# The attention stages in pairs of heads, and three of four value rows of one tile on TensorE

## What is computed

```python
def mla(q, k, v):                       # first block, causal
    s = q @ k.T / sqrt(96);  p = softmax(where(causal, s, -inf))
    return p @ v

def peer(x):                            # 128 experts per token
    s1, s2 = q[..., :64] @ keys_1.T, q[..., 64:] @ keys_2.T
    eidx, gates = top16_of_top16_by_top16(s1, s2)
    act = gelu(einsum('td,tkd->tk', x, peer_u[eidx]))
    return einsum('tk,tkd->td', gates * act, peer_v[eidx])

def nsa(q, ...):                        # second block, per head
    o_c = masked_softmax(q @ k_cmp.T / 8, cmp_end <= t) @ v_cmp   # 31 compressed keys
    o_s = masked_softmax(q @ k_sel.T / 8, causal) @ v_sel         # 512 tokens: every block is chosen
    o_w = masked_softmax(q @ k_win.T / 8, causal) @ v_win
    return g0 * o_c + g1 * o_s + g2 * o_w
```

## Time and profile before

| | us |
|---|---|
| median of the 3 runs shown | 3436.53 (3432.90 to 3439.03) |
| the profiled execution | 3432.37 |
| its span | 3431.0 |
| busy TensorE | 2454.4 (72%) |
| busy VectorE | 1890.6 (55%) |
| busy ScalarE | 456.1 (13%) |
| busy GpSimd | 1311.4 (38%) |

### The profile page before, as it was taken

One profiled execution on the slowest core, in us unless ns is written; L12 is line 12 of the kernel. 1 busy time (PEld: TensorE's weight loads), 2 busy tenths in 40 slices (PEclk: granted clock), 3 DMA queues, 4 the chain that ended last, 5 costly groups with the idle time before them and its releaser, 6 DMA issues. The chain is left out here.

```text
span 3431.0 us, 24950 instructions
## 1 busy us (share of the span) xinstructions
PE 2454.4 (72%) x8300; PEld 1594.3 (46%) x8300; DVE 1890.6 (55%) x3669; ACT 456.1 (13%) x1214; POOL 1311.4 (38%) x1041
## 2 busy tenths in 40 slices
PE   6998930365847543003959998897679979799989
PEld 3547630234526522002647686763356534466544
DVE  1511169887676778997777656666554442212100
ACT  1201000012101000000023210110122100122110
POOL 0000004767466877347664345885431241000000
PEclk9998965685767866555855579999755789855699
DMA  4221406898688999669897569999863699510176
GB/s 138 92 85 65 162 21 196 308 384 294 225 338 285 402 331 363 194 209 335 327 352 226 174 234 400 371 401 401 308 228 90 212 398 336 189 37 0 63 268 226
DMA packets 291711, 829.17 MB, mean 242 GB/s; under 512 B 23568, under 2 KB 30144, under 8 KB 290816
## 3 DMA queue, kind: packets, MB, share of 16 engines
q0 software_dynamic: 148416, 539.79, 43.8%
q1 hardware_dynamic: 139872, 283.19, 22.7%
q10 hardware_dynamic: 3296, 4.60, 0.4%
HBM read 825.40 MB, written 2.10 MB: 241 GB/s over the span
## 5 line engine op out<-in xcount | busy, mean ns | idle before, releaser
L306 POOL DMA_INDIRECT picks_rows<-peer_u_dram,expert x512 | 698.2, 1364 | 821.0 <-DVE expert L1441 506.1
L306 POOL DMA_INDIRECT picks_rows<-peer_v_dram,expert x512 | 605.7, 1183 | 770.1 <-DVE h L369 655.6
L363 DVE CUSTOM_DVE_ANT_0 picks_rows<-picks_rows,xn 128x1024 f32<-128x1024 f32 x512 | 616.7, 1223 | 178.8 <-DMA picks_rows<-peer_u_dram,expert 173.7
L369 DVE SCALAR_TENSOR_TENSOR h<-picks_rows,picks_weight,h 128x1024 f32<-128x1024 f32 x512 | 655.0, 1279 | 101.5 <-ACT aT L2031 47.7
L637 PE MATMUL psum<-identity_sb,n_scaled 128*128 128x128 f32 (+1 forms) x104 | 23.6, 405 | 327.0 <-DVE n_scaled L622 327.0
L447 PE MATMUL psum<-weight_ring,hnT 128*128 128x512 f32 (+4 forms) x576 | 238.6, 576 | 23.5 <-DMA weight_ring<-w_in_dram 11.9
L1727 PE MATMUL psum<-weight_ring,aT 128*128 128x512 f32 x512 | 224.4, 600 | 8.6 <-DMA weight_ring<-w_ff_dram 6.4
L931 DVE TENSOR_REDUCE na_negmax<-psum 128x1 f32<-128x15 f32 (+6 forms) x192 | 74.3, 387 | 254.6 <-PE psum L836 254.4
L835 PE MATMUL psum<-nsa_kT_sb,qT 64*128 64x128 f32 (+3 forms) x256 | 181.2, 809 | 0.0
L447 PEld LDWEIGHTS psum<-weight_ring,hnT 128*128 128x128 f32 (+1 forms) x576 | 106.9, 188 | 153.8 <-issue 140.4
L637 PEld LDWEIGHTS psum<-identity_sb,n_scaled 128*128 128x128 f32 (+1 forms) x104 | 19.4, 218 | 332.7 <-issue 293.0
(11 more groups left out here) (357 smaller groups left out, 3422.4 us busy)
## 6 DMA issues: line engine op xcount, KB each, us to landing
weight_ring<-w_ff_dram SPq DMA_DIRECT2D x48, 2048.0 KB, 16.0
weight_ring<-w_in_dram SPq DMA_DIRECT2D x44, 2048.0 KB, 13.2
weight_ring<-w_proj_nsa_dram SPq DMA_DIRECT2D x6, 2048.0 KB, 7.9
weight_ring<-w_out_dram SPq DMA_DIRECT2D x6, 2048.0 KB, 18.7
weight_ring<-w_ret_out_dram SPq DMA_DIRECT2D x4, 2048.0 KB, 7.9
weight_ring<-w_mix_out_dram SPq DMA_DIRECT2D x4, 2048.0 KB, 18.2
weight_ring<-w_peer_q_dram SPq DMA_DIRECT2D x4, 2048.0 KB, 13.2
picks_rows<-peer_u_dram,expert POOLq DMA_INDIRECT x512, 9.3
```

The source lines that it names most:

```text
L306: pool.indirect_dma_start(out=self.rows[:, n % GATHERS, :], out_offset=None, in_=table, in_offset=bass.IndirectOffsetOnAxis(ap=self.expert ...
L363: ins = nc.vector.tensor_tensor_reduce(out=row, in0=row, in1=self.x[t], scale=1.0, scalar=0.0, op0=ALU.mult, op1=ALU.add, accum_out=self.d ...
L369: ins = nc.vector.scalar_tensor_tensor(out=h, in0=row, scalar=self.weight[:, t % 2, k:k + 1], in1=h, op0=ALU.mult, op1=ALU.add)
```

## The change

**Attention.** Items come in pairs, two heads of the same tile and branch. The mask matmul is gone: q is scaled by a negative number, and VectorE adds a mask of 0 and large positive numbers to the scores in PSUM and takes the minimum in one operation (`tensor_tensor_reduce`, out in place). ScalarE's exponential has scale −1 and that minimum as bias. VectorE then takes the reciprocal of each row sum and scales the probabilities themselves, by the gate too. The value product is swapped: values are stationary (64 columns), the turned probabilities move (128 columns), and the output comes out turned, the two heads in the two halves of the partitions, all three branches summed in one PSUM bank; ScalarE copies a whole bank to `oT`. VectorE's output steps, the buffers `o` and `mla_o`, and the stages `to_…` and `to2_…` are gone. In the second block q, k and the compressed k stand on 128 partitions: head h has rows 64·(h%2) and up, which takes each k turned twice (`turn_twice`) and q turned in blocks of 128. Score banks are 4 (2 for more than 512 keys), probability buffers 4 and 4.

**Picks.** `on_pe` is true for three of four v picks of tile 1, 96 of 1024. For each GpSimd writes a diagonal matrix of weights (identity x weight, 128 x 128, four buffers, 5 picks behind the gathers), and TensorE adds the row by two matmuls of 512 columns to PSUM banks 6 and 7; `fold` adds the two banks to h at the end. Other stages have 6 banks now. The counts in `SHARES` are new, and picks are placed in finer turns in some stages. Up to `sel2` 399 − 17 = 382 picks are placed; `sel2`, `sel3` and `drain_0` take 51 + 51 + 28, of which 36 + 39 + 21 are TensorE's.

```diff
-BANKS = 8
+BANKS = 6
 SHARES = {
-    ... "ma2_1": 28, "ma3_1": 28, "rp_1": 43, "tr_1": 7, "re_1": 19, "rn_1": 8, "to_1": 4, "m1_1": 71, "mix_1": 24, ...
-    "sel2": 43, "sel3": 42, "drain_0": 28, ... "cmp2_0": 31, ... "na2_0": 89, "to2_0": 3, "m2_0": 42, ... "ff12_0": 61, "ff22_0": 60,
-    ... "cmp2_1": 17, ... "na2_1": 29, "to2_1": 1, "m2_1": 16, ... "ff12_1": 18, "ff22_1": 19, ...
+    ... "ma2_1": 26, "ma3_1": 27, "rp_1": 35, "tr_1": 7, "re_1": 58, "rn_1": 9, "m1_1": 55, "mix_1": 18, ...
+    "sel2": 51, "sel3": 51, "drain_0": 28, ... "cmp2_0": 41, ... "na2_0": 81, "m2_0": 46, ... "ff12_0": 50, "ff22_0": 49,
+    ... "cmp2_1": 24, ... "na2_1": 35, "m2_1": 10, ... "ff12_1": 11, "ff22_1": 12, ...
-def on_pe(k):
-    return False
+def on_pe(t, k):
+    return t == 1 and k % 4 > 0
...
+    def fold(self, dve, t):
+        ...
+        dve.wait_ge(self.taken["dve"], self.dve_done_by(end))
+        dve.wait_ge(self.taken["pe"], pe_picks)
+        for c, bank in enumerate(V_BANKS):
+            h = self.g.h[:, t, 512 * c:512 * c + 512]
+            self.g.nc.vector.tensor_tensor(h, h, self.g.psum[:, bank, :], ALU.add).then_inc(self.sum_added, 1)
...
+def turn_twice(g, bank, columns, src, rows):
+    for part in (0, HD):
+        mm = g.nc.tensor.matmul(g.psum[part:part + HD, bank, columns], src, g.identity[0:rows, 0:rows], start=True, stop=True)
...
-            nc.tensor.matmul(scores(i)[:, at:end], it.q, it.kT, start=True, stop=False)
-            return nc.tensor.matmul(scores(i)[:, end - it.bias.shape[1]:end], g.identity[:], it.bias, start=False, stop=True)
+        def value(pe, s):
+            for j in pair(s):
+                it = items[j]
+                pe.wait_ge(*s_copied.after(j + 1))
+                ...
+                for m, (_, keys, v) in enumerate(it.blocks):
+                    mm = nc.tensor.matmul(values(j), v, probsT[0:keys, j % 4, P * m:P * m + P], start=it.start and m == 0,
+                                          stop=it.stop and m == len(it.blocks) - 1)
+                mm.then_inc(s_values.sem, 1)
...
+            for s in range(steps + 2):
+                if wide:
+                    turn(pe, s - 1)
+                    score(pe, s)
+                else:
+                    score(pe, s)
+                    turn(pe, s - 1)
+                value(pe, s - 2)
+                g.picks.add(pe, 2 * min(s, steps))
...
+            for s in range(steps):
+                for i in pair(s):
                     dve.wait_ge(*s_scores.after(i + 1))
-                    nc.vector.tensor_reduce(negmax[:, i % 4:i % 4 + 1], scores(i), AX_X, ALU.max, negate=True).then_inc(s_max.sem, 1)
+                    nc.vector.tensor_tensor_reduce(out=scores(i), in0=scores(i), in1=items[i].mask, scale=1.0, scalar=-LOWEST,
+                                                   op0=ALU.add, op1=ALU.min, accum_out=least[:, i % 8:i % 8 + 1]).then_inc(s_least.sem, 1)
+                g.picks.use(dve)
+                for i in pair(s):
+                    it, p = items[i], probs[:, i % 4, 0:items[i].keys]
+                    f = factor[:, i % 8:i % 8 + 1]
+                    dve.wait_ge(*s_exp.after(i + 1))
+                    if it.seen is not None:
+                        nc.vector.tensor_tensor(p, p, it.seen, ALU.mult)
+                    link(nc.vector.reciprocal(f, rowsum[:, i % 8:i % 8 + 1]))
+                    ...
+                        ins = nc.vector.tensor_scalar(p, p, f, it.gate, ALU.mult, ALU.mult)
+                    ins.then_inc(s_normed.sem, 1)
                 g.picks.use(dve)
```

## The result

| | us |
|---|---|
| before, median of 4 | 3437.78 (3432.90 to 3445.01) |
| changed, median of 4 | 3163.11 (3153.72 to 3168.80) |
| ratio | 0.9197, 95% interval 0.9167 to 0.9227 |
| forecast | 3170, range 3100 to 3262 |

A forecast was written before the change was run, and what follows sets the result against it. Attention stages na2_0 to na2_2 were taken as TensorE's at 1.2 GHz, selection as VectorE's, ff22_0 and m1_1 as the DMA's. Terms −8 − 41 − 23 − 18 − 64 − 114 = −268 from 3432 gave 3164, rounded to 3170; range 3100 to 3262.

The forecast's parts named there:

- na2_2: Second block's last attention stage, no picks: masks go, paired scores overlap, clock rises to 1.00; 202 to 91 us, −111.
- na2_1: Second block's middle attention stage: VectorE's own work plus 35 picks, 108 us with gaps for 167, −59.
- na2_0: Second block's first attention stage: VectorE takes over as the bound, 208 us with gaps for 233, −25.
- To 519: Start of the kernel to 519 us: ma0_0 loses masks and output steps and to_0 goes, −8.
- sel2 to drain_0: Selection stages, 250 us: 96 picks go to GpSimd and TensorE, gathers 1.55 apart, 227 us, −23.
- GpSimd is the new bound: Rival for the selection: unpriced diagonals slow gathers to 1.9 to 2.2 us each, total 3210 to 3245; chance 0.12.
- my signs of being wrong: Listed signs included clock 0.50 in na2_2, minimum above 1.0 us, diagonals over 0.6 us, paired scores one after another.
- 519–1328: Stretch from 519 to 1328 us: fewer picks, masks gone, scores overlapping, to_1 gone, picks shifted (+7); −41.
- Second block, stages around: Stages around na2_0, 1578–2396: 22 more picks ahead +24, ff12_0 and ff22_0 −13; whole stretch −18.
- A cold attention: Rival: attention's clock stays at 1.2 GHz, na2_2 149 to 160 us, na2_1 118, total 3245; chance 0.18.
- an exposed chain: Rival: each attention step's chain of 3.7 us, passing VectorE twice, is not hidden; slower, above 3437; chance 0.04.
- no overlap: Rival: paired heads' scores do not overlap, 11.2 us a pair, +15 to +25, total 3190; within the forecast's 0.66.

The follow-up runs named there:

- split_pair: The changed kernel with each score of a pair on TensorE followed by the turn of one item, so the two scores stand apart: 3230.22 us, na2_2 114.0.
- mask_back: The changed kernel with the mask matmul put back behind each score on TensorE: 3229.09 us, na2_2 112.6.
- before_no_mask: The kernel before without its mask matmuls, masks left out of the result: 3352.03 us, na2_2 176.9.
- fill_start: The changed kernel with spare full-width matmuls on TensorE after the first and second step of each attention stage: 3152.11 us, ma0_0 31.5.
- act_diag: The changed kernel with the 96 diagonals made by ScalarE instead of GpSimd: 3118.60 us, ratio to before 0.9082, sel2 to drain_0 222.
- attn_only: The changed kernel with all picks on VectorE and the pick counts of the kernel before: 3175.15 us, ratio to before 0.9244.
- dve_picks: The changed kernel with its new counts but all 1024 picks on VectorE: 3174.16 us, ratio to before 0.9237, sel2 to drain_0 271.

## Why the prediction was right, and where it was wrong

**na2_2 (−111 forecast, −117).** The mechanism was right: the overlap of the halves, the high clock, three engines of nearly the same load. split_pair and mask_back each take away the neighbourhood of the scores and give back 29 and 28 us; the clock is 0.89 in the change. Of the sizes, the overlap is complete (1.13 for four against 1.12 for two), where I had taken 0.58 of the time; the steps cost 10.6 us per pair for 11. The minimum was 0.713 for the 0.69 that I had in my 0.77, and VectorE was busy for 54.02 us, not 60: an item costs 0.20 more than before, not 0.33. The clock came out as forecast, but my reason for it is only half tested. The masks were one of three causes that I named for the low clock, and before_no_mask says that taking them out is not enough: it is still 0.50 in na2_2. The lonely 64-row scores are back in split_pair, at 0.83. The transposes and value records behind each other are left of the three, and no run takes them away alone. The Trainium skill, "TensorE: Matmul & The Clock Gate", Part 4: PE-mode transpose, says that the higher clock does not engage for transposes, and I had 149 us for that case. The trace does not agree: the stage took 85 us at 0.89, with transposes back to back in every step, eight of 128 columns in 1.12 us.

**na2_1 (−59, −69) and na2_0 (−25, −49).** VectorE is the bound as forecast, although na2_0 kept a clock of 0.54. The sums were too long: 101 and 197 us of VectorE, 108 and 208 with gaps, where it is busy for 86.33 of 98 and 171.08 of 184. Wrong were both terms: its own records cover 48 and 78 us, not 53 and 86, and a pick is busy for 1.28, of which some overlaps with its neighbours' records, and does not take a pitch of 1.37.

**To 519 (−8, +10).** This is the step that failed in its sign. I let ma0_0 lose masks and output steps and kept its clock at 1.00, because it was there in the row. fill_start shows that the clock is what went wrong: with it ma0_0 takes 31.5 us and not 46.2, and sel0 ends at 508, 7 us earlier than in the kernel before, where I had 8. I had asked what the clock does where it was low and not where it was high.

**sel2 to drain_0 (−23, +12).** The term that failed is the diagonal: bounded by 0.25 and 1.3, it is 0.87 in the mean, and I took a spacing of 1.55 of gathers "as most of the diagonal is likely to fit into the issue gaps". Hardly any of it does: an issue gap behind a diagonal is 0.17 in place of 0.30, and otherwise the gathers' 0.95 to 0.99 and the diagonals' 0.62 to 1.26 stand behind each other, which makes the 7.34. The rival "GpSimd is the new bound" is what happened, at 1.83 per gather, between my forecast and its 1.9 to 2.2; with 1.83 in place of 1.55 the same sum gives 261 for the 262 measured (and at 2.2 it gives +56, not the +50 that I wrote). act_diag confirms it. Of my signs of being wrong, a diagonal over 0.6 us was there from the first one, 0.62. VectorE's own part was 95 and not 115, in dve_picks, where the sum is tested.

**519–1328 (−41, −58).** attn_only gives the split: −19 by the attention, where I had −25 with the turn stage, and −39 by the counts, where I had −23 and +7 for what moves within. That +7 is the term of the wrong size: m1_1 fell by 24, rp_1, mix_1 and others lost picks, and re_1, which takes 39 more, rose by only 28, less than 39 x 1.37 = 53, since they went into time in which VectorE had waited. My row of re_1 began at 997, but the stage begins at 964 with a wait of TensorE of 34 us; VectorE was busy for 63 us of its 86 and is now for 104 of 115.

**Second block, stages around.** −38 for −18 is na2_0's −49, +28 in the stages ahead of it (22 picks more, +24 forecast), and −15 in ff12_0 and ff22_0 (−13): VectorE ends ff22_0 with TensorE now, the 14 us behind it are gone.

**The rivals.** A cold attention did not come in na2_2; an exposed chain did not come: the waits of TensorE's weight loads on VectorE's scaled probabilities are 19.7 us in na2_2, spread over 18 places, and TensorE is idle for 11 of 85. What I had priced at +15 to +25 for "no overlap" is +29 in na2_2 alone and +67 in all, since na2_1 becomes TensorE's again (+31): the overlap was worth three times what I had put on it.

## What to carry to other kernels

Two matmuls that each use half of the rows of the array cost one if they stand side by side in opposite halves (1.13 us for four records against 1.12 for two), and in both runs that put a full matmul between them that was gone, at 66 and 67 us. So count what stands between two instructions, and not only their own time: the masks' own 16 us cost 28 in na2_2 because of where they stand. When an edit takes "useless" work off an engine, look at stages where the clock was high, too: ma0_0 lost 15 us once its masks were gone. Before a task is given to the engine that looks idle, add up its instruction's whole price, the waits behind its neighbour's operations too; another idle engine may do it for half (0.40 us on ScalarE, 0.87 on GpSimd).

## What the runs showed of the hardware

- Two score records of 64x512 of one head take 1.12 us at 2.4 GHz, and four of two heads in opposite halves of the rows 1.13.
- TensorE can be busy without pause and stay at 1.2 GHz: ma0_0 ran at 0.50 with TensorE busy for 35.94 of 36 us (46.2 us in all), and at 1.00 with six extra matmuls in its first 7 us (31.5).
- A diagonal of 128x128 takes GpSimd 0.62 us. One that starts while VectorE is inside an operation with two SBUF inputs ends 0.47 us after that operation, a gather 0.81 to 0.87 us after it (otherwise it takes 0.94 to 0.98), so the price hangs on when it starts. Value picks that started inside a diagonal took their usual 1.28. ScalarE makes a diagonal in 0.40.
- A minimum with a mask as second input and the result written back to PSUM costs 0.713 us for 512 columns, a plain maximum 0.690.
